# Linear attention: the keys are copied head by head, the first factor is made while their projection runs, and the weight rounding moves behind it

## The reference

```python
q, k, v, z, a_low = jnp.split(h @ w_in, ...)            # 4 heads, keys of 128, values of 256
log_a = jax.nn.log_sigmoid(a_low @ w_a2 + b_a) / 16.0    # one decay for each token and key column
# in each chunk of tokens, b = cumsum(log_a):
o_inter = einsum('bhik,bhkv->bhiv', qb * exp(b), state)
attn = einsum('bhik,bhjk,bhijk->bhij', qb, kb, exp(b_i - b_j))      # j <= i
o = o_inter + einsum('bhij,bhjv->bhiv', attn, vb)
state = exp(b_last) * state + einsum('bhjk,bhjv->bhkv', kb * exp(b_last - b), vb)
```

## Time and profile before

| | us |
|---|---|
| median of 3 runs | 2658.5 |
| the profiled execution's own time | 2659.2 |
| its span | 2656.9 |
| TensorE busy | 2488.1 |
| DVE busy | 1385.3 |
| ACT busy | 1070.0 |
| POOL busy | 255.9 |
| mean granted clock of TensorE | 0.966 of full speed |

### The profile page before, as it was taken

One profiled execution on the slowest core, in us unless ns is written; L12 is line 12 of the kernel. 1 busy time (PEld: TensorE's weight loads), 2 busy tenths in 40 slices (PEclk: granted clock), 3 DMA queues, 4 the chain that ended last, 5 costly groups with the idle time before them and its releaser, 6 DMA issues.

```text
span 2656.9 us, 32579 instructions
## 1 busy us (share of the span) xinstructions
PE 2488.1 (94%) x12787; PEld 2017.5 (76%) x12787; DVE 1385.3 (52%) x2380; ACT 1070.0 (40%) x1994; POOL 255.9 (10%) x420
## 2 busy tenths in 40 slices
PE   6889999999988989899989999999998999999998
PEld 4667777778745767788767888888876988888887
DVE  3567577565376555653235433325775785533322
ACT  4355343252444445643454322214436563422222
POOL 3234011102000013200000000001001120000000
PEclk9989999999989989999999999999997999999999
DMA  6522265246310331223111333223322000233322
GB/s 235 191 73 72 89 230 177 93 144 205 111 54 32 107 112 32 64 80 117 46 56 56 96 96 101 97 94 99 103 80 64 17 9 30 90 95 99 100 94 73
DMA packets 152624, 253.29 MB, mean 95 GB/s; under 512 B 15663, under 2 KB 72314, under 8 KB 151449
## 3 DMA queue, kind: packets, MB, share of 16 engines
q1 hardware_dynamic: 135408, 201.25, 24.0%
q0 software_dynamic: 14816, 48.31, 5.5%
q10 hardware_dynamic: 2249, 1.65, 0.2%
HBM read 248.99 MB, written 5.32 MB: 96 GB/s over the span
## 4 chain that ended last, share of the span: by engine, by line
PE 78%; DVE 9%; ACT 8%; DMA 3%; issue 2%; POOL 0%; ACTq 0%; DVEq 0%
PE PS L220 21%; PE PS L221 21%; PE PS L222 21%; PE PS L988 2%; ACT tmp L756 1%; DVE x L812 1%; PE PS L2411 1%; PE PS L2416 1%; PE PS L1819 1%; PE PS L1620 1%; PE PS L1607 1%; DMA mraw<-in_w_mod 1%; DVE w_lo L212 1%; DVE hT_lo L824 1%; DMA w_raw<-in_gla_w_in 1%
## 5 line engine op out<-in xcount | busy, mean ns | idle before, releaser
L212 DVE TENSOR_TENSOR w_lo<-w_raw,w_hi 128x1024 fp32r<-128x1024 f32 (+1 forms) x344 | 411.8, 1206 | 706.8 <-ACT w_hi L205 705.9
L205 ACT ACTIVATE w_hi<-w_raw 128x1024 fp32r<-128x1024 f32 (+1 forms) x344 | 356.0, 1045 | 966.8 <-DMA w_raw<-in_ffn_w_gate_up 304.0
L220 PE MATMUL PS<-hT_hi,w_hi 128*128 128x512 f32 (+1 forms) x1728 | 662.9, 384 | 21.0 <-DVE hT_lo L824 12.2
L221 PE MATMUL PS<-hT_lo,w_hi 128*128 128x512 f32 (+1 forms) x1728 | 654.2, 379 | 0.0
L222 PE MATMUL PS<-hT_hi,w_lo 128*128 128x512 f32 (+1 forms) x1728 | 654.1, 379 | 0.0
L220 PEld LDWEIGHTS PS<-hT_hi,w_hi 128*128 128x128 f32 x1728 | 332.1, 192 | 88.2 <-issue 20.6
L222 PEld LDWEIGHTS PS<-hT_hi,w_lo 128*128 128x128 f32 x1728 | 331.9, 192 | 59.9
L221 PEld LDWEIGHTS PS<-hT_lo,w_hi 128*128 128x128 f32 x1728 | 332.1, 192 | 55.9 <-issue 0.2
L220 PE MATMUL PS<-w_hi,hT_hi 128*128 128x512 f32 (+1 forms) x704 | 285.4, 405 | 32.5 <-DVE hT_lo L824 10.4
L221 PE MATMUL PS<-w_lo,hT_hi 128*128 128x512 f32 (+1 forms) x704 | 275.9, 392 | 0.0
L222 PE MATMUL PS<-w_hi,hT_lo 128*128 128x512 f32 (+1 forms) x704 | 275.5, 391 | 0.0
(11 more groups left out here) (587 smaller groups left out, 3229.5 us busy)
## 6 DMA issues: line engine op xcount, KB each, us to landing
w_raw<-in_ffn_w_gate_up SPq DMA_DIRECT2D x176, 256.0 KB, 3.1
mraw<-in_w_mod POOLq DMA_DIRECT2D x160, 256.0 KB, 4.0
w_raw<-in_gla_w_in SPq DMA_DIRECT2D x48, 512.0 KB, 4.7
w_raw<-in_ffn_w_down SPq DMA_DIRECT2D x44, 512.0 KB, 3.7
w_raw<-in_fox_w_in SPq DMA_DIRECT2D x32, 512.0 KB, 4.4
w_raw<-in_sgu_w_in SPq DMA_DIRECT2D x24, 512.0 KB, 4.9
w_raw<-in_dn_w_in SPq DMA_DIRECT2D x24, 512.0 KB, 3.6
w_raw<-in_gla_w_out SPq DMA_DIRECT2D x16, 512.0 KB, 4.8
```

The lines of the kernel that those rows point to most:

```text
L205: nc.scalar.activation(w_hi[:, n % NS, :, 0:m], w_raw[:, n % NS, :, 0:m], ACT.Copy).then_inc(w_hidone, 1)
L212: nc.vector.tensor_tensor(w_lo[:, n % NS, :, 0:m], w_raw[:, n % NS, :, 0:m], w_hi[:, n % NS, :, 0:m].bitcast(F32), ALU.subtract).then_inc( ...
L220: nc.tensor.matmul(o, l_hi, r_hi, start=start, stop=False)
L221: nc.tensor.matmul(o, l_hi, r_lo, start=False, stop=False)
```

## The change

The keys' projection signals each of the first three heads as its last matmul is issued (`k0`). ACT rounds only Z0.2 and Z0.3 ahead, takes the first exponential, and copies the keys in four instructions of 512 columns, each as its head is done; the second copy (head 2, whose bank the turned factor goes to) signals `lab`. DVE makes the first product between the sums of head 2 and head 3. Its rests of Z0.2 and Z0.3 move behind the products of level 1, those of V1.0 and V1.1 into levels 2 and 4; ACT's roundings of the last two move to levels 2 and 4 as well. TensorE waits for the first head's `b` instead of all four.

```diff
                 def part(b, forms, c):
-                    for form in forms:
+                    for n, form in enumerate(forms):
                         for k in range(CK):
                             mm = form_pass(...)
+                        if n < 3 and c == b.n - 1:
+                            mm.then_inc(q.k0, 1)
...
-                                pe_.wait_ge(q.b_done, GH * (j + 1))
+                                pe_.wait_ge(q.b_done, GH * j + 1)
...  ACT
-                act_feed(ahead(K))
-                a.wait_ge(w_used, K.last + 1)
-                a.activation(r.kT[:], PS[:, 0:4, :], ACT.Copy).then_inc(ps_evac, 1)
-                act_feed(ahead(K) + 1)
+                act_feed(ahead(K) - 1)
+                a.wait_ge(q.e, NE * GH * j + 1)
+                a.activation(r.E[:, 0, :], r.E[:, 0, :], ACT.Exp, scale=1 / 16).then_inc(q.ex, 1)
+                for n, h in enumerate((0, 2, 3, 1)):
+                    a.wait_ge(*((w_used, K.last + 1) if n == 3 else (q.k0, 3 * j + n + 1)))
+                    ins = a.activation(r.kT[:, h, :], PS[:, h, :], ACT.Copy)
+                    if n == 1:
+                        ins.then_inc(q.lab, 1)
+                ins.then_inc(ps_evac, 1)
...  ACT, in the loop of levels; level 0 of head 0 is left out there
+                        if h == 0 and l in (2, 4):
+                            act_feed(ahead(K) + l // 2 - 1)
...  DVE
-                v.wait_ge(q.lab, j + 1)
+                v.wait_ge(q.lab, 2 * j + 1)
                 for h, g in heads:
                     ... bias, subtraction, sums of head h ...
-                dve_feed(ahead(K))
-                dve_feed(ahead(K) + 1)
-                v.wait_ge(q.at0, j + 1)
-                v.wait_ge(ps_evac, K.ev)
+                    if h == 2:
+                        v.wait_ge(q.ex, NE * GH * j + 1)
+                        v.wait_ge(q.lab, 2 * j + 2)
+                        v.tensor_tensor(r.E[:, 0, :], r.E[:, 0, :], r.kT[:, 0, :], ALU.mult).then_inc(q.kq, 1)
...  DVE, in the loop of levels
                         ins.then_inc(q.kq, 1)
+                        if h == 0 and l == 1:
+                            dve_feed(ahead(K) - 1)
+                            v.wait_ge(q.at0, j + 1)
+                            v.wait_ge(ps_evac, K.ev)
                         copy_level(l - 1)
+                        if h == 0 and l in (2, 4):
+                            dve_feed(ahead(K) + l // 2 - 1)
```

More of the change, by code:

```diff
@@ L854, in trans_dve @@
             split(3)
-        gla_s = sig("gla", "lowTd wa2 lg lab b_done e ex kq pe_e dg cp kxs kv s o rstd on ot at0 dec qx fm fe szd")
+        gla_s = sig("gla", "k0 lowTd wa2 lg lab b_done e ex kq pe_e dg cp kxs kv s o rstd on ot at0 dec qx fm fe szd")
         def gla_layer(i, j):
@@ L1069, in act @@
                         c = NE * g + l
-                        a.wait_ge(q.e, c + 1)
-                        a.activation(r.E[:, c % 2, :], r.E[:, c % 2, :], ACT.Exp, scale=1 / 16).then_inc(q.ex, 1)
+                        if h or l:
+                            a.wait_ge(q.e, c + 1)
+                            a.activation(r.E[:, c % 2, :], r.E[:, c % 2, :], ACT.Exp, scale=1 / 16).then_inc(q.ex, 1)
+                        if h == 0 and l in (2, 4):
+                            act_feed(ahead(K) + l // 2 - 1)
                         if l == 0 and h:
@@ L1199, in dve @@
                         e = r.E[:, c % 2, :]
+                        if l == 0:
+                            if h:
+                                v.wait_ge(q.ex, c + 1)
+                                v.tensor_tensor(e, e, r.kT[:, h, :], ALU.mult).then_inc(q.kq, 1)
+                            continue
                         v.wait_ge(q.ex, c + 1)
-                        if l == 0:
-                            v.tensor_tensor(e, e, r.kT[:, h, :], ALU.mult).then_inc(q.kq, 1)
-                            continue
                         s = LEVELS[l - 1]
```

## The result

The changed kernel takes 2638.8 us, median of four runs (2637.26 to 2639.28), against 2658.13 for the kernel before beside it: a ratio of 0.9923, 95% interval 0.9905 to 0.994. The profiled execution takes 2638.6 us. The forecast was 2641 with a range of 2636 to 2649.

The account below looks back on a forecast made before the run. TensorE, busy 94% of the span, was taken as the bound, with its waits for head 0's first product in two layers. A ceiling of 21.8 us less 2.3, 0.8 and 0.7 gave 18.0, so 2641 us, range 2636 to 2649.

Parts of the forecast that it names:

- What bounds, and what goes: TensorE's wait for head 0's first product in both gla layers: 7.58 us idling and 2.42 low clock go in layer 0.
- the ceiling: Most that can be gained by level 7 of head 0: 11.2 us in layer 0, 10.6 in layer 3, 21.8 together.
- The first product and level 1: Head 0's first product ready 1.2 us before the keys' matmuls end; level 1's products ready 0.4 us before PE asks.
- The rests on DVE: Four rests between head 0's products add waits at levels 2 and 3: 2.3 us in layer 0, 0.8 in layer 3.
- Both engines at once: DVE's moved product and rests meet POOL's work of levels 1 to 3: 0.67 us lost for both layers, bounds 0 and 1.3.
- The sum: Whole kernel: 21.8 - 2.3 - 0.8 - 0.7 = 18.0 us gained, so 2641 us.
- A: Rival: DVE bounds head 0, all rests and three sums on the path; gain 9.7 us, 2649; chance 0.13.
- B: Rival: gain given back in head 1, waiting for weights landing at their old time; 6.5 us, 2647.5; chance 0.09.
- C: Rival: gaps at levels 2 and 3 lower the clock through head 0; slower, 2665; chance 0.06.
- D: Rival: the first product doesn't come before the projection's end and keeps its old place; 2658; chance 0.05.

Follow-up runs that it names:

- the gap filled: Kernel before, with 30 extra matmuls of 512 columns between the keys' projection and head 0; ratio 0.9977 to the kernel before.
- the late rests: Changed kernel with DVE's rests of V1.0 and V1.1 moved from levels 2 and 4 to the end of head 0; 2636.36 us, again 2636.38.
- the second traces: Kernel before and changed kernel each run again unedited; from the keys' last matmul to level 7, 31.85 and 25.12 us in layer 0, 31.39 and 22.55 in layer 3.
- The first comparison: Changed kernel against the kernel before, first time: 2638.8 us against 2658.13, ratio 0.9923; repeated unedited on another chip, 0.9943.
- the product behind the sums: Changed kernel with DVE's first product behind the sums of head 3, not between heads 2 and 3; 2643.82 us, ratio 0.9958.
- layer 0 alone: Changed order in layer 0 only, layer 3 as in the kernel before; 2648.93 us, ratio 0.9981 to the kernel before.

## Why the prediction was right

**What bounds, and what goes.** Right. The first product was held up by a rounding that it doesn't need, and for 2.8 us by the copy in one piece. Idling and low clock both went: with the gap filled, the way from the turn to level 1, for which the forecast took off 2.42 us of clock, shrank by 2.4 in layer 0 and 2.5 in layer 3. But the cadence that the ceiling takes for levels 1 to 7, 16.98 us, is one that no run reached. Where the rests stay in front of level 1, levels 2 to 7 take 14.98 us in layer 0 and 14.42 in layer 3 with none of the four rests or roundings among them (before: 15.20 and 14.42); the ceiling has 14.04. So the ceiling of the gain was 0.9 and 0.4 us too high.

**The first product and level 1.** Right. The product runs from 125.77 to 126.46 and is ready 1.3 us before the last keys' matmul ends (127.75); the forecast said 1.2. Level 1's products are ready when PE asks, with no wait.

**The rests on DVE.** The places were right in layer 0, levels 2 and 3; in layer 3 they are levels 2 and 4. The waits in brackets were forecast at 1.2 and 1.1 us and are 1.50 and 1.38. Measured from level to level, levels 1 to 4 of layer 0 take 4.65, 3.91 and 3.42 us, against a cadence of 2.94, 2.28 and 2.94: 3.8 us more, where the sum had 2.3.

**Both engines at once.** This term was mis-sized, 0.7 us for both layers. The products of a level took 0.76 us in the sum; DVE's rows show 0.72 + 0.41 at level 2 and 0.76 + 0.83 at level 4, and the sum of the modulation 1.16 instead of 0.74. Each of the long ones overlaps POOL's differences. POOL pays as well. Its pair for level 4 of layer 3, in the changed kernel and then with the late rests:

```profile
982.96 1.58 POOL L1139 TENSOR_TENSOR gla_E<-gla_b 128x256 f32<-128x256 f32 x1 [0.89 <-PE PS L990]
984.50 1.19 POOL L1140 TENSOR_TENSOR gla_E<-gla_b 128x256 f32<-128x256 f32 x1
```

```profile
980.95 0.77 POOL L1139 TENSOR_TENSOR gla_E<-gla_b 128x256 f32<-128x256 f32 x1 [0.88 <-PE PS L990]
981.67 0.79 POOL L1140 TENSOR_TENSOR gla_E<-gla_b 128x256 f32<-128x256 f32 x1
```

The first pair takes 2.8 us and holds up ACT's exponential, for which DVE waits 1.17 us. The run with the late rests takes one rest from beside that pair: the pair takes 1.6 us, and level 3 to level 4 takes 3.05 us, not 3.48. POOL's instructions are the same, only DVE's queue differs, so what makes this pair slow is the work beside it on DVE. For the other slow rows that is read from the overlap alone; no run took POOL's work away.

The stretch was forecast at 23.1 us in layer 0 (3.47 + 16.98 + 2.3, and 0.39 for the last matmul) and 21.6 in layer 3, and is 25.1 and 22.5. That is 2.8 us more, where the sum had 0.7 for this term. Of the 2.8, the ceiling's 0.9 and 0.4 us above are the cadence, which the forecast took from two levels. The other 1.5 us are left for what DVE and POOL do at once, by this subtraction and not by a run.

**The sum.** 18.0 us were forecast, and by the traces the change itself gives 15.9 (15.6 between the second traces). Level 7 was to come 8.5 to 9 us sooner in layer 0 and about 9.5 in layer 3; counted from the keys' last matmul it comes 6.9 and 9.0 sooner. The change gave less than forecast, and yet the time came out 2 us below the forecast: that it lies so near is in part luck. The first comparison gave 20.5 us (15.9 to 25.3), the second 15.1 (11.9 to 18.6), and neither interval excludes 15.9 or 18.

**The rivals.** A (all rests on the path, 9.7 us) did not come, though in layer 0 DVE is busy for 20.7 of the 21.4 us over these levels: it is nearly the bound. B: nothing was given back; counted from the last keys' matmul, head 3's turn, some 80 us behind level 7, comes 7.3 us sooner in layer 0 (104.6 us, 111.9 before). Head 1's two long waits, 2.63 and 3.84 us before, are 2.63 and 1.44 (2.62 and 2.99 in the second trace, against 2.63 and 4.23). C: the clock stayed at 1.00 in the window over the two waits. But the evidence on which it was dismissed was weaker than it read: 2.63 us of idling left the clock high. The changed kernel's head 1 has the same gap and pays:

```profile
172.12 2.05 PE L990 MATMUL PS<-gla_E 128*128 128x128 f32 x8 [2.63 <-DVE gla_E L1219]
```

These eight matmuls take 2.05 us, not 1.13 (the granted clock is 0.50 from 172 to 176 us), and 1.86 us were enough in the run with the product behind the sums. D did not come.

## What to carry to other kernels

Look at what stands in front of the operand that the longest wait names: here two engines' queues held work there whose own input landed later and whose user was some 40 us off. Move that work into a later wait of the same engine, not into the next steps: at the end of head 0 two of the rests cost nothing. Price work that is moved on DVE with its durations beside a busy POOL, take the cadence from all the levels and not from the best, and count the low clock behind a gap as part of the gap.

## What the runs showed of the hardware

Whether the clock falls behind a short idle time can't be told from its length alone in these traces: 1.4 and 1.5 us left it high, 1.86 lowered it once. Behind the gap of 2.63 us in head 1 the eight matmuls took 2.05 and 2.04 us in the two traces of the changed kernel, 1.13 in both of the kernel before, and 1.13 in the run with layer 0 alone, whose layer 0 is the changed one.

Two executions of one program differ by up to 3 us in their first 96 us: the changed kernel by 2.95, with granted clocks of 1.00 and 0.85 between 24 and 34 us, the kernel before by 1.56, with 0.83 and 1.00.

VectorE and GpSimd slow each other in overlapping `tensor_tensor` work in float32: a pair of GpSimd differences took 2.8 us where a VectorE rest overlapped its start and 1.6 where that rest had been moved away, and a VectorE product of 128x256 took 0.41 us by itself and 0.72 to 0.83 beside such differences.
